# Latent attention: scores on a ring of four banks, transposes on a ring of two, and four smaller changes beside it

## What is computed

```python
for l in range(2):
    h = rmsnorm(x, norm_mix_g[l])
    if l == 0:   # pooled groups, gated convolution, layer norm, silu
        gl = glu_a * sigmoid(glu_b)
        cv = causal_dwconv(gl, dw_w) + dw_b            # 31 taps, 512 columns
        yb = silu(layernorm(cv, ln_g, ln_b))
        x = x + concat([ya, yb]) @ w_out
    else:        # latent attention, 16 heads
        cq, ckv, k_pe = split(h @ w_dq_dkv)
        q = rmsnorm(cq) @ w_uq; k_nope, v = split(rmsnorm(ckv) @ w_ukv)
        p = softmax(where(causal, (q_nope k_nope + rope(q_pe) rope(k_pe)) * scale, -1e30))
        x = x + (p @ v) @ w_o
    m = rmsnorm(mem, norm_mem_g[l])                    # 256 memory rows
    k, v = split(m @ xa_wkv[l])                        # 1024 columns each
    x = x + softmax(xq k / 16) v @ xa_wo[l]
    x = x + conv_ffn(rmsnorm(x, norm_ffn_g[l]))
shift, scale, gate = split(silu(c) @ w_ada + b_ada)    # 3 x 1024 values
h = rmsnorm(x, norm_g) * (1 + scale) + shift
x = x + gate * (attentions(h @ w_in) @ w_out); return rmsnorm(x, final_g)
```

## Time and profile before

| what | us |
|---|---|
| median of 3 runs (lowest to highest) | 1738.78 (1738.09 to 1739.87) |
| the profiled execution's own time | 1737.93 |
| its span in the trace | 1736.2 |
| TensorE busy | 1697.1 (98%) |
| VectorE busy | 1055.0 (61%) |
| ScalarE busy | 696.0 (40%) |
| mean granted TensorE clock of the span | 0.997 of full |

### The profile page before, as it was taken

One profiled execution on the slowest core, in us unless ns is written; L12 is line 12 of the kernel. 1 busy time (PEld: TensorE's weight loads), 2 busy tenths in 40 slices (PEclk: granted clock), 3 DMA queues, 4 the chain that ended last, 5 costly groups with the idle time before them and its releaser, 6 DMA issues.

```text
span 1736.2 us, 21057 instructions
## 1 busy us (share of the span) xinstructions
PE 1697.1 (98%) x8009; PEld 1375.7 (79%) x8009; DVE 1055.0 (61%) x1516; ACT 696.0 (40%) x1124; POOL 23.3 (1%) x42
## 2 busy tenths in 40 slices
PE   8999999999999999999989999999999999999998
PEld 6888788788888888887657878888888887887776
DVE  5798354465555542378774645655555776357695
ACT  6221342543333332255672453433332112156574
POOL 1000000000000000001000000000000000000000
PEclk9999999999999999999999999999999999999999
DMA  6256232032222323211103202322226642321201
GB/s 194 85 169 194 67 103 97 25 97 97 97 97 97 97 86 114 85 65 42 49 1 122 98 25 97 97 96 96 95 97 204 216 141 72 99 83 44 73 25 49
DMA packets 154294, 164.40 MB, mean 95 GB/s; under 512 B 2998, under 2 KB 150383, under 8 KB 153967
## 3 DMA queue, kind: packets, MB, share of 16 engines
q1 hardware_dynamic: 153408, 162.51, 29.0%
q0 software_dynamic: 336, 0.53, 0.2%
q10 hardware_dynamic: 479, 0.39, 0.1%
HBM read 160.01 MB, written 3.15 MB: 94 GB/s over the span
## 4 chain that ended last, share of the span: by engine, by line
PE 84%; DVE 9%; ACT 4%; issue 1%; DMA 1%; SPq 0%; DVEq 0%; ACTq 0%
PE bank L914 83%; DVE cv L2205 3%; ACT xa_p L1613 1%; ACT mla_p L1613 1%; DVE w_lo L2095 1%; DMA x_nat<-in_x_dram 1%; DVE h_lo L2095 1%; ACT w_hi L1613 1%; PE bank L1321 0%; DVE nmax L2588 0%; DVE mla_q L2563 0%; DVE xa_pT_lo L2095 0%; ACT fb L1613 0%; DVE mla_q L2549 0%; DVE fb L2672 0%
## 5 line engine op out<-in xcount | busy, mean ns | idle before, releaser
L914 PE MATMUL bank<-h_hi,w_hi 128*128 128x512 f32 x1472 | 579.0, 393 | 5.4 <-DVE w_lo L2095 3.0
L914 PE MATMUL bank<-h_hi,w_lo 128*128 128x512 f32 x1472 | 573.4, 390 | 0.0
L914 PE MATMUL bank<-h_lo,w_hi 128*128 128x512 f32 x1472 | 573.0, 389 | 0.0
L2095 DVE TENSOR_TENSOR w_lo<-w_raw,w_hi 128x2048 fp32r<-128x2048 f32 (+6 forms) x138 | 276.9, 2011 | 242.6 <-ACT w_hi L1613 242.3
L1613 ACT ACTIVATE w_hi<-w_raw 128x2048 fp32r<-128x2048 f32 (+6 forms) x138 | 231.6, 1683 | 393.8 <-PE bank L914 388.3
L914 PEld LDWEIGHTS bank<-h_hi,w_hi 128*128 128x128 f32 x1472 | 276.1, 188 | 72.6 <-issue 8.9
L914 PEld LDWEIGHTS bank<-h_hi,w_lo 128*128 128x128 f32 x1472 | 276.1, 188 | 58.5
L914 PEld LDWEIGHTS bank<-h_lo,w_hi 128*128 128x128 f32 x1472 | 276.2, 188 | 57.8 <-issue 1.2
L914 PE MATMUL bank<-g_hi,w_hi 128*128 128x512 f32 x352 | 137.6, 391 | 0.0
L914 PE MATMUL bank<-g_hi,w_lo 128*128 128x512 f32 x352 | 137.0, 389 | 0.0
L914 PE MATMUL bank<-g_lo,w_hi 128*128 128x512 f32 x352 | 137.0, 389 | 0.0
(11 more groups left out here) (362 smaller groups left out, 2002.4 us busy)
## 6 DMA issues: line engine op xcount, KB each, us to landing
w_raw<-in_ffn_w_up_dram SPq DMA_DIRECT2D x44, 1024.0 KB, 5.1
w_whole<-in_xa_wkv_dram SPq DMA_DIRECT2D x16, 1024.0 KB, 5.4
w_raw<-in_ffn_w_down_dram SPq DMA_DIRECT2D x16, 1024.0 KB, 5.2
w_raw<-in_w_in_dram SPq DMA_DIRECT2D x13, 1024.0 KB, 5.3
ada_w<-in_w_ada_dram SPq DMA_DIRECT2D x12, 1024.0 KB, 7.7
w_raw<-in_xa_wq_dram SPq DMA_DIRECT2D x8, 1024.0 KB, 5.2
w_raw<-in_xa_wo_dram SPq DMA_DIRECT2D x8, 1024.0 KB, 5.1
w_raw<-in_pc_w_in_dram SPq DMA_DIRECT2D x6, 1024.0 KB, 5.5
```

The lines of the kernel that those rows point to most:

```text
L914: return nc.tensor.matmul(o, w, v, start=start, stop=stop, **kw)
L2095: return tt(lo_, v, hi.bitcast(f32), SUB)
```

## The change

**Latent attention.** A score unit takes the next of the banks 2, 3, 1, 6, and waits for the exponentials of the unit four before it in place of three. A transposed unit takes the next of banks 4 and 5, and waits for the copy of the unit two before it. A head's third transposed unit is issued behind the first score unit of the next head, or behind the query tile B or C, and VectorE's maxima and copies follow that order. In pair 5 the next pair's first score unit is issued ahead. Tile A of the second group goes to bank 7.

**Memory values of layer 1.** Slabs 4 to 7 of kv1 are split and multiplied in three parts (memory_values). The normed memory m1 is split for it by eight instructions on ScalarE and eight on VectorE. EARLY names slabs 4 and 5 of kv1. ScalarE's split of pc_out's first slab stands behind kv_out of slab 7.

**Layer norm.** VectorE adds the four column blocks, and later their squares (three additions each, two of them into a buffer used before), and TensorE makes one product with ones for each sum, behind slab 3 and behind slab 4.

**The rest.** keep_warm and its 18 products are gone. The last group of ada_columns stands behind spread, and mod[16:24] is made by VectorE at the norm's fourth tile. The load of the pooling weights counts on the semaphore small_loaded.

```diff
-    return ORDER[n][0] in ("kv0", "kv1")
+    return ORDER[n][0] == "kv0" or ORDER[n][0] == "kv1" and ORDER[n][1] < 4
...
-EARLY = [AT["pc_out", 0], AT["pc_out", 1]]
+EARLY = [AT["kv1", 4], AT["kv1", 5]]
...
-        def s_place(i):
-            return bank[(2, 3, 2, 1)[i]][:, 3 * P if i == 0 else 0:4 * P if i in (0, 3) else (i + 1) * P]
-
-        def t_place(j):
-            return bank[(4, 5, 6, 5)[j]][:, 3 * P if j == 3 else 0:(4, 3, 2, 4)[j] * P]
+        S_RING, UNIT_OF = (2, 3, 1, 6), (1, 2, 1, 0)
+
+        def s_bank(h, i):
+            return bank[S_RING[(3 * h + UNIT_OF[i]) % 4]]
+
+        def t_bank(h, u):
+            return bank[4 + (3 * h + u) % 2]
+
+        def s_free(h, u):
+
+            v = 3 * h + u - 4
+            return 4 * (v // 3) + (1, 3, 4)[v % 3]
...
+            def memory_values(s):
+                n = AT["kv1", s]
+                pe.wait_ge(lo_done, splits_before(n) + 1)
+                if s == 4:
+                    pe.wait_ge(mem_lo, DT)
+                wh, wl = view(w_hi[pair_of(n)], DT, 256), view(w_lo[pair_of(n)], DT, 256)
+                for j in range(2):
+                    c = slice(j * P, (j + 1) * P)
+                    slab_tile("kv1", n, 2 * s + j, kv_place(16 + 2 * s + j), DT,
+                              lambda k: (m1_hi[:, k, c], m1_lo[:, k, c]), lambda k: (wh[:, k, :], wl[:, k, :]), free=False)
...
-                memory(1, s)
+                if s < 4:
+                    memory(1, s)
+                else:
+                    memory_values(s)
...
+                if s == 3:
+                    pe.wait_ge(y_lo, 4)
+                    pe.wait_ge(ln_added, 3)
+                    mm(bank[4][:, :], ones[:, :], pool_a[:, 0:T], True, True).then_inc(ln_summed, 1)
                 if s == 4:
-                    pe.wait_ge(y_lo, 4)
-                    for i in range(4):
-                        pe.wait_ge(cv_ready, i + 1)
-                        mm(bank[4][:, :], ones[:, :], cv[:, i, :], i == 0, i == 3).then_inc(cv_summed, 1)
-                if s == 5:
-                    for i in range(4):
-                        pe.wait_ge(xc_sq, i + 1)
-                        mm(stat[:, :], ones[:, :], sq[i % 2][:, :], i == 0, i == 3).then_inc(xc_summed, 1)
+                    pe.wait_ge(ln_added, 6)
+                    mm(stat[:, :], ones[:, :], sq[0][:, :], True, True).then_inc(ln_summed, 1)
...
+                for u in units:
+                    unit = S_UNITS[u]
+                    if 3 * h + u == 3:
+                        pe.wait_ge(tile_free, mla_free("K", 5))
+                    elif 3 * h + u > 3:
+                        pe.wait_ge(lexp_done, s_free(h, u))
...
+                for u in units:
+                    if 3 * h + u > 1:
+                        pe.wait_ge(lt_done, 3 * h + u - 1)
...
             for pair in range(MH // 2):
                 first, second, g = 2 * pair, 2 * pair + 1, (pair + 2) // 2
                 if pair + 1 < MH // 2:
-                    scores(first + 2)
+                    scores(first + 2, (1, 2) if ahead(pair - 1) else (0, 1, 2))
                 if pair:
                     values(pair - 1)
                 else:
                     pe.wait_ge(tile_free, mla_free("A", 1))
-                turn(first)
+                turn(first, (0, 1))
                 if pair in (2, 4):
                     pe.wait_ge(tile_free, mla_free("C", g))
                     mla_tile("A", g)
                 if pair + 1 < MH // 2:
-                    scores(second + 2)
-                turn(second)
+                    scores(second + 2, (0,))
+                turn(first, (2,))
...
+                elif pair + 2 < MH // 2:
+                    scores(second + 3, (0,))
+                    turn(second, (2,))
+                else:
+                    turn(second, (2,))
...
-            keep_warm(bank[5], 5, 4 * P, ident_b[:, :], later_b[:, :])
             spread(bank[6], fb[0], 3 * NB)
-            keep_warm(bank[5], 9, 4 * P, ident_b[:, :], later_b[:, :])
+            ada_columns(ADA // 2 - 1)
...
-                if s == 4:
+                if s == 0:
+                    pooled_out((0, 1))
+                    for i in range(DT):
+                        a(m1_hi[:, i, :], m1[:, i, :], ACT.Copy).then_inc(m1_done, 1)
+                if s == 2:
+                    pooled_out((2, 3))
+                if s in (1, 3, 4, 5):
+                    split(AT["kv1", {1: 4, 3: 5, 4: 6, 5: 7}[s]])
+                if s == 3:
                     for i in range(4):
                         act.wait_ge(xc_ready, i + 1)
-                        wait(act, xc_summed, i - 1)
-                        a(sq[i % 2][:, :], cv[:, i, :], ACT.Square).then_inc(xc_sq, 1)
-                if s == 5:
-                    split(FIRST["pc_out"])
-                    act.wait_ge(xc_summed, 4)
+                        if i == 3:
+                            act.wait_ge(ln_added, 4)
+                        a(xc_square(i), cv[:, i, :], ACT.Square).then_inc(xc_sq, 1)
+                if s == 4:
+                    act.wait_ge(ln_summed, 2)
                     a(rstd[:, :], stat[:, :], ACT.Sqrt, scale=1.0 / (4 * P), bias=eps[:, :]).then_inc(ln_sqrt, 1)
                     for i in range(4):
                         act.wait_ge(ln_norm, i + 1)
                         a(cv[:, i, :], cv[:, i, :], ACT.Silu, scale=param("conv_ln_g", i),
                           bias=param("conv_ln_b", i)).then_inc(ln_silu, 1)
+            split(FIRST["pc_out"])
...
             pooled_out((0, 1))
-            conv(6)
+            dve.wait_ge(cv_ready, 2)
+            tt(pool_a[:, 0:T], cv[:, 0, :], cv[:, 1, :], ADD).then_inc(ln_added, 1)
+            conv(len(todo))
+            for i in (2, 3):
+                dve.wait_ge(cv_ready, i + 1)
+                dve.wait_ge(ln_added, i - 1)
+                tt(pool_a[:, 0:T], pool_a[:, 0:T], cv[:, i, :], ADD).then_inc(ln_added, 1)
             pooled_out((2, 3))
-            conv(len(todo))
-            dve.wait_ge(cv_summed, 4)
+            for i in range(DT):
+                dve.wait_ge(m1_done, DT + i + 1)
+                low(m1_lo[:, i, :], m1[:, i, :], m1_hi[:, i, :]).then_inc(mem_lo, 1)
+            split(AT["kv1", 4])
+            dve.wait_ge(ln_summed, 1)
             for i in range(4):
-                dve.wait_ge(cv_ready, i + 1)
                 stt(cv[:, i, :], bank[4][:, :], -1.0 / (4 * P), cv[:, i, :], MUL, ADD).then_inc(xc_ready, 1)
-            split(FIRST["pc_out"])
+            split(AT["kv1", 5])
...
+            for i in range(1, 4):
+                dve.wait_ge(xc_sq, i + 1)
+                wait(dve, ln_added, 2 + i)
+                tt(sq[0][:, :], sq[0][:, :], xc_square(i), ADD).then_inc(ln_added, 1)
+            split(AT["kv1", 6])
             dve.wait_ge(ln_sqrt, 1)
             link(nc.vector.reciprocal(rstd[:, :], rstd[:, :]))
             for i in range(4):
                 tt(cv[:, i, :], cv[:, i, :], rstd[:, :], MUL).then_inc(ln_norm, 1)
+            split(AT["kv1", 7])
+            split(FIRST["pc_out"])
...
+                    maxima(second + 2, (0,))
+                    turned(first, (2,))
+                    maxima(second + 2, (1, 2))
+                elif pair < MH // 2:
+                    turned(first, (2,))
                 if pair < MH // 2:
-                    turned(second)
+                    turned(second, (0, 1))
                 if pair + 1 < MH // 2:
                     sums(second + 2)
                 if pair in UQ_SPLIT:
...
+                elif pair % 2 and g < 3:
                     query_turn(g + 1)
+                    turned(second, (2,))
+                elif pair < MH // 2:
+                    turned(second, (2,))
...
+                if i == 3:
+                    dve.wait_ge(ada_cols, ADA // 2)
+                    tt(mod[:, 16:24], ada_sum[:, 16:24], prm[:, 1, 16:24], ADD)
```

More of the change, by code:

```diff
@@ L989, in _ @@
             nc.tensor.transpose(bank[0][:, 0:16], prow[0:16, 0, :], ident[0:16, 0:16]).then_inc(mixg_ready, 1)
-            keep_warm(bank[7], 4, 2 * P, ones[:, :], ones[:, :])
             def turn_x(i):
@@ L1170, in cross_attention, with ada_columns @@
                     outputs(h)
+            def ada_columns(pair):
+                pe.wait_ge(ada_added, 2 * DT * (pair + 1))
+                for j in range(4):
+                    c, v = 4 * pair + j, (pair % 4 * 4 + j) * P
+                    m = mm(ada_sum[:, c:c + 1], ada_acc[:, v:v + P], ones[:, 0:1], True, True)
+                m.then_inc(ada_cols, 1)
             def ffn(layer):
@@ L1184, in ffn @@
                     up_step(it)
-                def ada_columns(pair):
-                    pe.wait_ge(ada_added, 2 * DT * (pair + 1))
-                    for j in range(4):
-                        c, o = 4 * pair + j, (pair % 4 * 4 + j) * P
-                        m = mm(ada_sum[:, c:c + 1], ada_acc[:, o:o + P], ones[:, 0:1], True, True)
-                    m.then_inc(ada_cols, 1)
                 def down_slabs(slabs, it):
```

(9 more changed lines are left out.)

105 lines of the change are left out of this document (55 added, 50 removed).

## The result

The changed kernel takes 1743.36 us (median of 12 runs, 1740.15 to 1745.80) against 1738.56 us for the kernel before (12 runs, 1736.83 to 1741.25): ratio 1.0025, interval 1.0017 to 1.0034, so 3.0 to 5.9 us slower. The profiled run was the fastest of the twelve, 1740.15 us with a span of 1738.4, 2.2 us over the span before.

The account below looks back on a forecast made before the run. TensorE's stream and its few waits were taken to bound the kernel (busy 1697.1 of 1736.2 us). Terms +0.4, +1.65, +1.1 and -0.3 summed to +2.85, so 1741.6 us on the median scale, range 1735.5 to 1747.0.

Parts of the forecast that it names:

- kv1 and pc_out: Memory values and layer norm: pc_out 1.35 us earlier, low clock 1.75 us; +0.4 us in sum.
- the start: Program start without the four products: slower transposes 1.2 us, half-clock first products 0.45; +1.65 us (0.85 to 2.5).
- The two waits: TensorE waits for ScalarE's splits: 3.1 us before kv1's slab 7, 4.7 us before pc_out.
- the clock behind the waits: At pc_out: one low-clock stretch behind the wait there, costing half its length, 1.75 us.
- my upper bound: Memory values and layer norm: +2.2 us, if slab 7's wait brings a low stretch of its own.
- idle time lowers the clock at more places: Rival: slab 7's wait and one in latent attention bring a low stretch each, 3.5 us; 1745.1 us, chance 0.25.
- Latent attention: Latent attention: 8.1 us of waits for exponentials go, 9.2 us for copies come; +1.1 us (-8.1 to +3).
- The reading by pairs: Latent attention: third copies wait 2.8 us in pairs 0 and 2, 1.4 in pair 4; last pair 2.2.
- the ring works as meant: Rival, latent attention: the 8.1 us of waits go and none comes; 1732.4 us, chance 0.15.
- The step that failed: Start: twelve transposes of x at half clock take longer and delay what follows by 1.2 us.
- the sign I had named for being wrong: Start: the prediction is wrong if no granted clock falls there.
- Norm: Second block's norm: moved column sums -0.9, spread -0.5, missing fillers +1.1; -0.3 us (-1.4 to +1.5).

Follow-up runs that it names:

- after_fillers: The changed kernel with all eighteen products without a reader put back, at the start and around spread; ratio 1.0010 to the kernel before.
- after: The changed kernel whole, against the kernel before: 1743.36 us, ratio 1.0025; its trace is of the fastest run, 1740.15 us.
- mem_only: The kernel before with only the memory values in three parts and the layer-norm sums added on VectorE; ratio 1.0010.
- mem_mended: mem_only with ScalarE's split of slab 7 ahead of the silu and pc_out's behind slab 6's result; 1732.05 us, ratio 0.9950 to the kernel before.
- third_first: best plus the attention part, with the third unit ahead of tile B and its copy ahead of split and query pair; ratio 0.9968 to the kernel before.
- ring_only: The kernel before with rings of four and two banks in latent attention, units in the old order; 1749.61 us, ratio 1.0053.
- start_only: The kernel before without the four products ahead of the transposes of x; ratio 1.0010.
- norm_only: The kernel before without the fourteen products around spread and with the last column sums behind spread; ratio 0.9997.
- ln_only: The kernel before with layer-norm sums added on VectorE, memory values whole, pc_out's split directly behind slab 4's result; ratio 1.0018.
- after_mended: The changed kernel with ScalarE's two splits moved as in mem_mended; 1734.44 us, ratio 0.9960 to the kernel before.
- best: mem_mended plus the last column sums behind spread, all fillers kept, latent attention as before; 1730.45 us, ratio 0.9945 to the kernel before.
- mla_only: The kernel before with only the latent attention part of the change (banks, order of units, waits); ratio 0.9999.

## Why the prediction was right, and where not

The time lay in the range, on the slower side of the forecast: +4.8 us by the medians (3.0 to 5.9 by the ratio's interval) against +2.85. In the traces the sum is +2.23 against +2.85, and that closeness is partly luck: kv1 and pc_out came 2.4 us above their term, the start 2.6 us below its own.

**kv1 and pc_out: mechanism right, size wrong.** The two waits came at the places named, and their lengths within 0.2 us. In after_fillers, which had no low clock at slab 7, pc_out started 64.40 us behind kv1's first product, 1.43 less than before, where I had 1.35; in after, with it, 65.94, 0.11 more than before. The term that failed is the clock behind the waits. I put one low stretch of 3.5 us into the sum and a second one in front of slab 7 among the bounds and rivals; there were three, 10.2 us in all: one at slab 7, two around pc_out's start. Measured +2.84, and my upper bound was +2.2. mem_only showed it again, after_fillers with the two at pc_out only, and mem_mended that it goes with the waits. What I priced as a rival ("idle time lowers the clock at more places") is what happened here, at one of the two places I named. The Trainium skill ("TensorE: Matmul & The Clock Gate", "Why this matters for your kernels") warns of gaps between bursts of products; the trace agrees in kind, with low clock behind waits of 2.92 and 4.60 us, though after_fillers had the shorter wait and no low clock behind it.

**Latent attention: right in sum.** +0.74 us against +1.1 in the trace, at the same low-clock time. Exponentials' waits went wholly; waits for copies rose from 2.7 us (1.5 and 1.2, the other rows of that view before) to 11.0, by 8.3 where I had 9.2, and the one for mla_q, which I hadn't counted, by 1.0. The reading by pairs was only partly right: I put most of it, 7.0 us, on the third copy behind split and query pair; the values products waited 5.3 us, and third_first moved that without a gain. The two banks cost it, as ring_only shows. The rival "the ring works as meant" fell.

**Start: not settled.** +1.65 forecast, -0.99 in the trace. The step that failed is that the transposes at half rate would push the first weight product: it waits for VectorE (1.21 us) and for x's load, so they had cover. I had also taken full rate for all transposes before, from the two later groups of the earlier trace rows; the first eight took 0.22 us each. And the sign I had named for being wrong, no fall of the granted clock at the start, can't decide: both traces show 1.00 from 0 to 20 us, over products and transposes that ran at half pace. start_only allows 0 to 3.3 us. after_fillers gives 2.6 us for all fillers, of which the norm has 1.45 to 1.9 by traces; what remains for the start is about 1 us, an estimate with an interval as wide as itself.

**Norm: right by luck.** -0.28 against -0.3 in the trace after, but +0.30 in norm_only, which has the same edit. The terms came as -1.15 for the moved sums (I had -0.9, and -0.5 for spread) and +1.45 to +2.4 for the missing fillers (I had +1.1). The last of them was too small: I had the clock back within the first tile, and it stayed low for 10.2 us in all three traces without fillers.

**The clock's scatter: missed.** I read one trace and took its low stretches as fixed. The unchanged latent attention has one to four of them, worth up to 5 us, and the runs of the kernel before lie between 1736.7 and 1746.2 us, so that single traces of two kernels say little about a change of 2 us unless the low-clock time is compared first. What decides how many come in a run isn't settled by these runs.

## What to carry to other kernels

Work taken off the busiest engine is only worth what the next wait leaves of it: write down in order what the helper engine has in front of each operation that the busiest engine will need sooner, and move those first. The same removal here made its two stages 2.7 us slower or 8.6 faster, by two splits' places on ScalarE's list. When two traces differ by a few us, compare the granted clock stage by stage ahead of any cause.

## What I had not expected of the hardware

Away from the program's end, low clock came in pieces of 3.4 us in every trace, each worth up to 1.7 us, and the same instructions with the same waits had one piece in one run and four in another (120.30 and 125.28 us). The wait of 4.60 us was followed by two pieces in all three traces that had it, that of 2.92 us by one in two of the three; ln_only's wait of 4.79 us came with two as well. Around the second block's norm, the three traces without fillers (after, after_mended, norm_only) had 10.2 us of low clock, and the eleven with them 3.4 us (eight) or none (three: after_fillers, best, mla_only); the fillers were worth 1.45 to 2.4 us of the last stretch. At the program's start the granted clock reads 1.00 in both traces while transposes take 0.22 us each and later ones 0.14, so there the length of the products says more than that column.
